# Hybrid decoder trunk, mixer projections: state space recurrence in steps of two tokens, and the input projection's units in another order with v, z and all six gates as three rounded products

## The chip, the cores and the metric

One core of one Trainium2 chip. The time is device microseconds of one execution. "Half step" below is one 128-token half of a 512-column projection; PE is TensorE, DVE VectorE, ACT ScalarE, POOL GpSimd, SP the queue that loads the weights.

## The reference

Two decoder layers on 256 tokens of width 1024, float32. Each layer first computes h = RMSNorm(x) and one wide projection of h, whose column blocks are:

```python
IN_SIZES = (MOBA_WIDTH, MOBA_WIDTH, MOBA_WIDTH,      # q, k, v of block attention, 512 each
            SSM_WIDTH,                               # u of the state space branch, 512
            GDN_WIDTH, GDN_WIDTH, GDN_WIDTH,         # q, k, v of gated DeltaNet before its convolution
            GDN_HEADS, GDN_HEADS, GDN_WIDTH,         # ab (8 columns), z
            D_MODEL, D_MODEL, D_MODEL)               # three merge gates, 6 blocks of 512
```

The state space branch keeps, for each of 32 groups of 16 channels, a complex diagonal state of 64:

```python
_, h = lax.associative_scan(combine, (a_elems, bu), axis=1)     # h_t = Lbar h_(t-1) + Bbar u_t
y = jnp.einsum('gnp,bsgp->bsgn', c_mat, h).real
y = y + d_skip * uf                                              # then GELU and GLU
```

Block attention and gated DeltaNet (GDN: a chunked delta rule with the inverse of a 64x64 unit lower triangle for each chunk and head) are the two other branches. The gated sum of the three goes through an output projection, then cross-attention and a feed-forward part follow (dense in layer 0, 8 experts in layer 1).

## The kernel before

The program is written out by hand: each engine has its own list of instructions, and semaphores join the lists. A list is worked through in order, so an instruction that waits holds back all that stand behind it on its engine.

**Weights.** SP loads 2 MB units of weights (24 a layer in the mixer, `mixer_units`, L74) into a ring of three slots; unit j is loaded when unit j - 3 has been multiplied (`multiplied`, L463). The first 14 units are column blocks of the input projection: u, q, k, v, z, gates 0 to 2, then the three convolution blocks QG, KG, VG, then the `NLATE` = 3 late units, gates 3 to 5.

**Two ways to multiply.** A float32 product of 128x128 by 128x512 is two PE instructions (`tokens_out` L2308, `features_out` L2295, `fill` L2365). A late unit (`late_gate` L2385) is multiplied as three rounded (fp32r) products: ACT writes the rounded weights (`unit_split_hi` L947), DVE the rest of them in place of the raw weights (`unit_split_lo` L1486), and h is parted in the same way (`h_rest` L1563, whose result lies over h itself, so that it waits until all float32 readers of h are done). A product is then h_hi x w_hi + h_lo x w_hi + h_hi x w_lo. Each unit is parted in four groups of 128x1024.

**State space loop.** 16 pairs of groups are worked in 8 steps g (`NGS` = 8). For each step PE makes B u into two PSUM banks of a pair that alternates (`s5_in` L2414), DVE turns it by a table of angles, scans it over 256 tokens and turns it back (L1618 to L1651), and PE multiplies the state by C (`s5_out` L2428). Tables are made four groups at a time by POOL (`angle_table` L812) and ACT (`table` L1006). After every second step DVE does `gelu_in(q-1)` (L1611), which waits for `s5_out` of two steps (y_read). PE's order around it is

```python
for g in range(NGS):
    s5_in(g)
    fill(4 + 2 * g)
    fill(5 + 2 * g)
    if g > 0:
        s5_out(g - 1)
s5_out(NGS - 1)
for f in range(F_LATE, NFILL):
    late_gate(f)
```

so that 16 half steps (v, z, gates 0 to 2, QG, KG, VG) stand in the loop and the three late units behind it. ACT takes each half step out of its bank, DVE turns q and k by position (L1592 to L1608) and scales the convolution's input (`conv_scale` L1556). Before the loop, `turn_b` (L2350) and `turn_c` transpose the matrices B and C, and `b_copy` and `c_copy` (L1016, L1022) bring them to SBUF.

**GDN inverse.** Six levels k double the size of the inverted blocks. Each level multiplies M_k by Z (L2612), ACT copies the product W (L1228), PE multiplies W with X and Z (L2621, L2624), DVE subtracts (L1866); one or two products for the cross-attention's values (`memory_values` L2548) stand between levels. M_k is masked by POOL (L855).

## Time and profile before

| | us |
|---|---|
| median of 3 runs (1904.75 to 1908.10) | 1907.74 |
| the profiled execution | 1899.46 |
| its span, first to last instruction | 1897.70 |
| PE busy / DVE busy / ACT busy / POOL busy | 1804.3 / 1410.7 / 1012.4 / 228.0 |
| state space loop and late units, layer 0 | 66.92 to 226.83 |
| the same, layer 1 | 700.58 to 860.48 |
| GDN inverse, layer 0 | 312.46 to 339.73 |
| expert part of layer 1 | from about 1110 to the end |

A line of the timeline reads: start, duration, engine, line of the kernel, operation, output<-inputs, shape, count of merged instructions, and in brackets the idle time before it and what ended it. Durations of one instruction reach beyond the start of the next where an engine is pipelined; the distance from start to start is what it costs.

### The profile page before, as it was taken

The numbers are of one execution on the slowest core, as the hardware profiler recorded it, in microseconds if no ns is written. First come the engines' busy times: TensorE is split into PE (matmuls) and PEld (weight loads), VectorE is DVE, ScalarE is ACT, GpSimd is POOL, SyncE is SP. The second block draws the span as 40 slices with busy tenths as digits, with TensorE's granted clock in tenths as the row PEclk, the third lists the DMA queues.
The fourth block names the chain that finished last, engine by engine and source line by source line (L and its number), as shares of the span: only waits on it lengthen the run. The fifth ranks groups of instructions, "written<-read, shape, count | busy, mean of one in ns | idle before, by whom it ended". The sixth has DMA issues, their size and how long they took to land.

```text
span 1897.7 us, 22679 instructions
## 1 busy us (share of the span) xinstructions
PE 1804.3 (95%) x9095; PEld 1369.5 (72%) x9095; DVE 1410.7 (74%) x1643; ACT 1012.4 (53%) x1164; POOL 228.0 (12%) x227
## 2 busy tenths in 40 slices
PE   7999999998999999998999879999999999999995
PEld 5447767576888744686766768787878787878784
DVE  4798778345555359986855469898989898989895
ACT  4231555345444312244714557777777777777773
POOL 9560001010000248100010010000000000000010
PEclk9999999999999999999999989999999999999998
DMA  7333422057553433343303469999999999999992
GB/s 246 133 133 133 178 89 90 1 208 246 199 183 105 150 133 133 133 155 112 131 4 144 145 249 391 379 390 359 390 361 390 361 390 355 391 354 392 353 392 86
DMA packets 204567, 434.85 MB, mean 229 GB/s; under 512 B 6888, under 2 KB 45936, under 8 KB 204464
## 3 DMA queue, kind: packets, MB, share of 16 engines
q1 hardware_dynamic: 196464, 414.20, 60.1%
q0 software_dynamic: 5136, 17.01, 2.5%
q10 hardware_dynamic: 2864, 2.23, 0.4%
q8 instruction: 69, 1.13, 0.2%
q14 instruction: 34, 0.28, 0.0%
HBM read 422.93 MB, written 10.49 MB: 228 GB/s over the span
## 4 chain that ended last, share of the span: by engine, by line
PE 80%; DVE 11%; ACT 5%; issue 2%; DMA 1%; ACTq 0%; POOL 0%; DVEq 0%; SPq 0%
PE bank L2749 14%; PE bank L2751 14%; PE bank L2750 14%; PE bank L2310 10%; PE bank L2381 4%; DVE split_e L1496 3%; PE bank L2303 2%; PE bank L2326 2%; PE bank L2330 2%; PE bank L2327 2%; PE bank L2551 2%; DVE phase L1745 1%; PE bank L2403 1%; PE bank L2409 1%; PE bank L2405 1%
## 5 line engine op out<-in xcount | busy, mean ns | idle before, releaser
L1496 DVE TENSOR_TENSOR split_e<-ring,split_e 128x2048 fp32r<-128x2048 f32 x264 | 600.4, 2289 | 50.9 <-ACT split_e L973 50.6
L973 ACT ACTIVATE split_e<-ring 128x2048 fp32r<-128x2048 f32 x264 | 503.8, 1919 | 160.6 <-PE bank L2751 159.1
L2749 PE MATMUL bank<-split_e,fx_e 128*128 128x512 f32 x704 | 278.8, 396 | 2.0 <-DVE fx_e L2163 2.0
L2751 PE MATMUL bank<-split_e,fx_e 128*128 128x512 f32 x704 | 274.7, 390 | 0.0
L2750 PE MATMUL bank<-split_e,fx_e 128*128 128x512 f32 x704 | 274.2, 389 | 0.0
L2310 PE MATMUL bank<-ring,hT 128*128 128x512 f32 x448 | 199.3, 603 | 3.1 <-DVE uT L1553 3.1
L2310 PEld LDWEIGHTS bank<-ring,hT 128*128 128x128 f32 x448 | 85.3, 193 | 108.8 <-issue 108.8
L2749 PEld LDWEIGHTS bank<-split_e,fx_e 128*128 128x128 f32 x704 | 132.2, 188 | 28.2 <-DVE fx_e L2163 2.2
L2751 PEld LDWEIGHTS bank<-split_e,fx_e 128*128 128x128 f32 x704 | 132.1, 188 | 28.2
L2750 PEld LDWEIGHTS bank<-split_e,fx_e 128*128 128x128 f32 x704 | 132.4, 188 | 26.3
L2749 PE MATMUL bank<-split_e,f_actT_e 128*128 128x512 f32 x352 | 138.7, 394 | 9.2 <-DVE f_actT_e L2171 9.2
L2750 PE MATMUL bank<-split_e,f_actT_e 128*128 128x512 f32 x352 | 137.1, 389 | 0.0
L2751 PE MATMUL bank<-split_e,f_actT_e 128*128 128x512 f32 x352 | 137.1, 389 | 0.0
L2749 PEld LDWEIGHTS bank<-split_e,f_actT_e 128*128 128x128 f32 x352 | 66.1, 188 | 26.1 <-DVE f_actT_e L2171 12.8
L2381 PE MATMUL bank<-hT,ring 128*128 128x256 f32 x384 | 84.5, 381 | 0.0
L2381 PEld LDWEIGHTS bank<-hT,ring 128*128 128x128 f32 x384 | 72.5, 190 | 11.6 <-issue 2.0
L2751 PEld LDWEIGHTS bank<-split_e,f_actT_e 128*128 128x128 f32 x352 | 66.1, 188 | 13.9
L2750 PEld LDWEIGHTS bank<-split_e,f_actT_e 128*128 128x128 f32 x352 | 66.1, 188 | 13.2
L1490 DVE TENSOR_TENSOR ring_r<-ring,ring_r 128x1024 fp32r<-128x1024 f32 x46 | 54.8, 1221 | 18.4 <-ACT ring_r L962 18.1
L2749 PE MATMUL bank<-split_mix,fx 128*128 128x512 f32 x168 | 66.5, 396 | 1.7 <-DVE phase L2106 1.7
L2751 PE MATMUL bank<-split_mix,fx 128*128 128x512 f32 x168 | 65.6, 390 | 0.0
L2750 PE MATMUL bank<-split_mix,fx 128*128 128x512 f32 x168 | 65.4, 389 | 0.0
(545 smaller groups left out, 3138.3 us busy)
## 6 DMA issues: line engine op xcount, KB each, us to landing
ring<-in_moe_w_gate SPq DMA_DIRECT2D x40, 2048.0 KB, 11.4
ring<-in_moe_w_up SPq DMA_DIRECT2D x40, 2048.0 KB, 11.3
ring<-in_moe_w_down SPq DMA_DIRECT2D x40, 2048.0 KB, 11.7
ring<-in_w_in SPq DMA_DIRECT2D x28, 2048.0 KB, 7.9
ring<-in_ffn_w_gate SPq DMA_DIRECT2D x11, 1024.0 KB, 5.4
ring<-in_ffn_w_up SPq DMA_DIRECT2D x11, 1024.0 KB, 8.0
ring<-in_ffn_w_down SPq DMA_DIRECT2D x11, 1024.0 KB, 8.7
ring<-in_ssm_w_glu SPq DMA_DIRECT2D x8, 1024.0 KB, 6.2
```

The costliest lines, as they stand in the source:

```text
L973: nc.scalar.activation(split_e[j % NBUF][:, HI, :], ring[:, s * PIECE + i * HGRP:s * PIECE + (i + 1) * HGRP], ACT.Copy).then_inc(split_hi, 1)
L1490: V.tensor_tensor(unit_lo(j, i), unit_raw(j, i), unit_hi(l, m).bitcast(F32), ALU.subtract).then_inc(split_lo, 1)
L1496: V.tensor_tensor(split_e[j % NBUF][:, LO, :], ring[:, s * PIECE + i * HGRP:s * PIECE + (i + 1) * HGRP], split_e[j % NBUF][:, HI, :].bitca ...
L2303: last = mm(B[banks[m // 2]][:, (m % 2) * SEQ:(m % 2 + 1) * SEQ], w[:, k, m * P:(m + 1) * P], src[:, k, :], start=k == 0, stop=k == KD - 1)
L2310: last = mm(B[bank][:, :], src[:, k, t * P:(t + 1) * P], w[:, k, n0:n0 + 512], start=k == 0, stop=k == kt - 1)
L2326: mm(B[bank][:, :], a[LO], hi, start=k == 0, stop=False)
L2327: freed = mm(B[bank][:, :], a[HI], hi, start=False, stop=False)
L2330: last = mm(B[bank][:, :], a[HI], lo, start=False, stop=k == 4 * per_group - 1)
L2381: last = mm(B[t][:, (m % 2) * SEQ:(m % 2 + 1) * SEQ], w[:, k, m * P:(m + 1) * P], hT[:, k, :], start=k == 0, stop=k == KD - 1)
L2749: mm(bank, a[HI], w[HI], start=first, stop=False)
L2750: mm(bank, a[HI], w[LO], start=False, stop=False)
L2751: return mm(bank, a[LO], w[HI], start=False, stop=last_one)
```

## The change

It does these things, in both layers unless said otherwise:

1. **Two tokens a step.** The scan runs over 128 pairs of tokens (`HS` = 128) with the decay squared. u is stored with the even tokens first and the odd ones behind. The input of a pair is B2 u_even + B u_odd, with B2 = Lbar B, a second matrix (`b_pad2`, `bT2`). States of odd tokens are read out with C; even tokens from the state before, with C2 = C Lbar (`cT2`, made by `output_matrix` on DVE), and with a direct term C B (`d_mat`, made by `direct` on PE and `d_copy` on ACT). Tables, scans and all DVE operations of a step are half as wide. B u now always goes to banks 6 and 7.
2. **Another order.** Units: u, q, k, QG, KG, VG, v, z, gates 0 to 5. `NLATE` is 8: v, z and the six gates are multiplied in three rounded passes, and five of the eight stand inside the loop, from step 3 on. The buffers of the rounded weights are four for all late units: group i of a unit is rounded when PE has used group i of the unit before.
3. **Layer 1 only:** q and k too are multiplied in three rounded passes (`early_hi`, `EARLY_HI`).
4. **GDN inverse:** level 0 takes M_0 and its product straight (X and Z begin as the identity), and level 5 leaves out the product that makes X.

```diff
@@ units
-    NLATE = 3
+    NLATE = 8
+    HS = 128
-        return ([in_cols(l, c) for c in (IN_U, 0, 512, 1024, IN_Z)]
-                + [in_cols(l, IN_GATE + 512 * g) for g in range(6 - NLATE)]
-                + [in_cols(l, c) for c in (IN_QG, IN_KG, IN_VG)]
-                + [in_cols(l, IN_GATE + 512 * g) for g in range(6 - NLATE, 6)]
+        return ([in_cols(l, c) for c in (IN_U, 0, 512, IN_QG, IN_KG, IN_VG, 1024, IN_Z)]
+                + [in_cols(l, IN_GATE + 512 * g) for g in range(6)]
@@ POOL
...
                 nc.gpsimd.memset(b_pad[:, :, :, :, :], 0.0).then_inc(pad_ready, 1)
+                nc.gpsimd.memset(b_pad2, 0.0).then_inc(pad_ready, 1)
@@ ACT
+            def early_hi():
+                for half in range(2):
+                    ks = slice(half * (KD // 2), (half + 1) * (KD // 2))
+                    nc.scalar.activation(e_r[HI][:, ks, :], hT[:, ks, :], ACT.Copy).then_inc(x_hi, 1)
+                    if U_LATE < j < U_GLU:
+                        act.wait_ge(split_used, unit_splits(l) + m - 4 + 1)
+                    early_hi()
+                    unit_split_hi(l, U_Q, range(4))
...
+                if l > 0:
+                    unit_split_hi(l, U_Q + 1, range(4))
-                b_copy(l)
+                b_copy(l, bT, 6, 1)
                 c_copy(l)
+                b_copy(l, bT2, 2, 3)
+                d_copy(l)
                 table(l, 0)
...
+                for n_ in range(NLATE):
+                    unit_split_hi(l, U_LATE + n_ + 1, range(4))
+                    late_out(n_)
+                    if n_ == 1:
+                        table(l, NQ - 1)
+                    if n_ == NGS - 4:
+                        for q in range(NQ):
+                            gelu_tanh(q)
@@ DVE, constants (each 128x32)
+            V.tensor_copy(AI, c_[6])
+            V.tensor_scalar(AR, c_[7], 1.0, None, ALU.add)
+            link(V.tensor_tensor(BCI, c_[11], c_[8], ALU.mult))
+            V.tensor_tensor(c_[8], BCR, AR, ALU.mult)
...
+            V.tensor_tensor(BCI2, c_[10], c_[11], ALU.add).then_inc(s5_const, 1)
@@ DVE, layer 1 before u: e_lo twice, then unit_split_lo(U_Q); after u: unit_split_lo(U_Q + 1)
+                input_matrix(0, b_pad, BCR, BCI)
+                input_matrix(1, b_pad2, BCR2, BCI2)
@@ DVE, end of a step of the loop
                     if g % 2 == 0:
                         dve.wait_ge(h_rot, n + 1)
                         if q > 0:
                             gelu_in(q - 1)
+                    if g == 0:
+                        output_matrix()
+                    if g == 2:
+                        unit_split_lo(l, U_LATE, range(4))
+                        dve.wait_ge(fill_ready, NFILL * l + F_LATE)
+                        h_rest(0)
+                        h_rest(1)
+                    if g >= 3:
+                        unit_split_lo(l, U_LATE + g - 2, range(4))
@@ DVE, GDN levels
+                        if k == 0:
...
+                            V.tensor_tensor(XZ[:, t, 0], XZ[:, t, 0], M_lvl[0][:, t], ALU.subtract)
...
+                            V.tensor_tensor(XZ[:, t, 1], XZ[:, t, 1], ps, ALU.subtract).then_inc(xz_ready, 1)
+                            continue
@@ PE
+                def late_unit(n_):
...
+                    for i in range(4):
+                        m = FIRST_SPLIT[j] + i
+                        pe.wait_ge(split_lo, unit_splits(l) + m + 1)
+                        if n_ == 0 and i % 2 == 0:
+                            pe.wait_ge(x_lo, xs_base(l) + X_H + i // 2 + 1)
+                        for t in range(NT):
+                            at, bank = slice(t * P, (t + 1) * P), B[2 * (n_ % 2) + t]
+                            for k in (2 * i, 2 * i + 1):
+                                hi, lo = (...)
+                                mm(bank[:, :], h_lo[:, k, at], hi, start=k == 0, stop=False)
+                                freed = mm(bank[:, :], h_hi(k)[:, at], hi, start=False, stop=False)
+                                last = mm(bank[:, :], h_hi(k)[:, at], lo, start=False, stop=k == KD - 1)
+                def direct():
+                    pe.wait_ge(bct_ready, 4 * l + 3)
+                    for q in range(NQ):
+                        for i in range(NQ):
+                            a = 32 * i
+                            for c in range(2):
+                                last = mm(B[2][a:a + 32, q * 32:(q + 1) * 32],
+                                          b_pad[:, c, NQ * q + i].rearrange("p g n -> p (g n)"), cT[:, c, q, a:a + 32],
+                                          start=c == 0, stop=c == 1)
                 def s5_in(g):
-                        pe.wait_ge(bu_read, NS5 * l + 2 * g - 2)
+                        pe.wait_ge(bu_read, NS5 * l + 2 * g)
                     for c in range(2):
                         for j in range(2):
-                            last = mm(s5_bank(g, j)[:, c * SEQ:(c + 1) * SEQ], bT[a:a + 32, c, q, :], uT[a:a + 32, q, :], ...)
+                            mm(s5_bank(g, j)[:, c * HS:(c + 1) * HS], bT2[a:a + 32, c, q, :], uT[a:a + 32, q, 0:HS],
+                               start=True, stop=False)
+                        for j in range(2):
+                            last = mm(s5_bank(g, j)[:, c * HS:(c + 1) * HS], bT[a:a + 32, c, q, :], uT[a:a + 32, q, HS:SEQ], ...)
                 def s5_out(g):
+                            mm(y[r_, 0:HS], cT2[:, c, q, r_], h[:, j, c, 0:HS], start=c == 0, stop=False)
+                        mm(y[r_, 0:HS], d_mat[r_, q, :], uT[r_, q, 0:HS], start=False, stop=True)
+                            last = mm(y[r_, HS:SEQ], cT[:, c, q, r_], h[:, j, c, 1:HS + 1], start=c == 0, stop=c == 1)
-                turn_b()
+                turn_b(0, b_pad, 6)
                 turn_c()
+                turn_b(1, b_pad2, 2)
                 fill(3)
+                direct()
                 for g in range(NGS):
                     s5_in(g)
-                    fill(4 + 2 * g)
-                    fill(5 + 2 * g)
+                    if g < 3:
+                        fill(4 + 2 * g)
+                        fill(5 + 2 * g)
+                    if g > 3:
+                        late_unit(g - 3)
                     if g > 0:
                         s5_out(g - 1)
+                    if g == 3:
+                        late_unit(0)
                 s5_out(NGS - 1)
-                for f in range(F_LATE, NFILL):
-                    late_gate(f)
+                for n_ in range(NGS - 3, NLATE):
+                    late_unit(n_)
@@ PE, GDN levels
-                    for t in range(NT):
+                    for t in range(NT) if k > 0 else ():
...
-                        for h, b, r_ in blocks:
+                        for h, b, r_ in blocks if k < 5 else ():
```

## Rows read from the trace of the kernel before

**Rows 1.** The page, part 4: the chain that ended last, by engine and line

```profile
PE 80%; DVE 11%; ACT 5%; issue 2%; DMA 1%; ACTq 0%; POOL 0%; DVEq 0%; SPq 0%
```

**Rows 2.** Busy time of each engine over loop and late units, layers 0 and 1

```profile
core 0: us, PE busy (x) PEld busy (x) DVE busy (x) ACT busy (x) POOL busy (x), PEclk, DMA share, GB/s
66.92:226.83 159.91, 159.91 (x625) 101.50 (x625) 141.57 (x198) 47.54 (x57) 55.53 (x24) 1.00 0.41 145
700.58:860.48 159.90, 159.90 (x625) 101.50 (x625) 142.04 (x198) 47.59 (x57) 55.96 (x24) 1.00 0.41 145
```

**Rows 3.** Timeline of PE in layer 0, loop and late units

```profile
58.22 1.04 PE L2354 MATMUL bank<-ident,b_pad 128*128 128x128 f32 x8
...
66.92 1.13 PE L2424 MATMUL bank<-uT,phase 32*128 32x256 f32 x8
67.99 14.00 PE L2310 MATMUL bank<-ring,hT 128*128 128x512 f32 x32
81.92 1.13 PE L2424 MATMUL bank<-uT,phase 32*128 32x256 f32 x8
...
96.91 1.06 PE L2438 MATMUL bank<-phase 128*32 128x256 f32 x8
```

**Rows 4.** The same timeline, first late product and what follows the last

```profile
194.05 0.50 PE L2403 MATMUL bank<-ring_r,m_hi 128*128 128x512 f32 x1
...
226.83 1.91 PE L2469 MATMUL bank<-ident,qk 128*128 128x128 f32 x16
```

**Rows 5.** Timeline of DVE in layer 0: gelu_in twice, and the parting

```profile
119.55 1.01 DVE L1616 TENSOR_SCALAR ring<-ring 128x256 f32<-128x256 f32 x1
...
178.15 0.48 DVE L1613 SCALAR_TENSOR_TENSOR yT<-uT,params,bank 128x256 f32<-128x256 f32 x1 [4.74 <-PE bank L2438]
178.67 0.42 DVE L1615 TENSOR_TENSOR ring<-yT 128x256 f32<-128x256 f32 x1
179.13 0.29 DVE L1616 TENSOR_SCALAR ring<-ring 128x256 f32<-128x256 f32 x1
...
179.80 0.68 DVE L1632 TENSOR_TENSOR phase<-bank,phase 128x512 f32<-128x512 f32 x1
...
190.10 4.63 DVE L1490 TENSOR_TENSOR ring_r<-ring,ring_r 128x1024 fp32r<-128x1024 f32 x4
194.65 1.22 DVE L1567 TENSOR_TENSOR merged_hi<-hT,m_hi 128x1024 fp32r<-128x1024 f32 x1
```

**Rows 6.** Timeline of POOL: first and last operation of one angle table

```profile
112.36 2.15 POOL L820 TENSOR_TENSOR ring<-s5c,steps 128x1024 f32<-128x1024 f32 x1 [4.55 <-ACT phase L1014]
...
130.70 1.29 POOL L827 TENSOR_SCALAR ring<-ring 128x1024 f32<-128x1024 f32 x1
```

**Rows 7.** Busy time by stretches, as rows 2: PE's two longest waits after the start

```profile
292.95:295.73 2.78, 0.00 (x2) 0.00 (x1) 2.71 (x4) 2.78 (x7) 0.00 (x0) 1.00 0.02 7
...
1095.40:1101.85 6.45, 0.00 (x0) 0.00 (x0) 4.00 (x28) 1.88 (x4) 0.00 (x0) 0.54 1.04 408
1101.85:1109.60 7.75, 6.49 (x30) 6.42 (x31) 3.34 (x7) 0.00 (x0) 0.00 (x0) 0.50 0.07 26
```

**Rows 8.** Timeline of PE in layer 1 before the loop

```profile
669.76 22.27 PE L2310 MATMUL bank<-ring,hT 128*128 128x512 f32 x48 [1.33 <-DVE uT L1553]
...
693.62 7.03 PE L2310 MATMUL bank<-ring,hT 128*128 128x512 f32 x16
```

**Rows 9.** Timeline of DVE in layer 0 ahead of the first half step

```profile
30.54 1.97 DVE L1541 TENSOR_SCALAR cosr<-cosr 128x64 f32<-128x64 f32 x1
```

**Rows 10.** Timeline of PE in layer 0: GDN inverse, levels 0 and 1

```profile
312.46 1.37 PE L2612 MATMUL bank<-uT,ring 64*64 64x64 f32 x32 [0.49 <-POOL ring L855]
313.71 0.68 PE L2621 MATMUL bank<-uT,ring 64*64 64x64 f32 x16
314.20 0.66 PE L2624 MATMUL bank<-ring,uT 64*64 64x64 f32 x16
...
315.73 1.12 PE L2551 MATMUL bank<-ring,hT 128*128 128x512 f32 x2
316.78 1.15 PE L2612 MATMUL bank<-uT,ring 64*64 64x64 f32 x32
```

**Rows 11.** The page, part 6: loads of the input projection's units

```profile
ring<-in_w_in SPq DMA_DIRECT2D x28, 2048.0 KB, 7.9
```

More of the change, by code:

```diff
@@ L228, in hybrid_trunk @@
         r5 = Region(phase, PH)
-        tab = [r5.take(NQ, 2, SEQ) for _ in range(2)]
+        r5.take(1024)
+        b_pad2 = r5.take(2, NS5, 2, 16)
         bT, cT = r5.take(2, NQ, P), r5.take(2, NQ, P)
-        s5_m1, s5_m2, s5_in_rot = (r5.take(2, 2, SEQ) for _ in range(3))
-        s5_h = [r5.take(2, 2, SEQ) for _ in range(2)]
-        ang, turns = spare_half(0, 0), spare_half(0, 1)
-        s_half = spare_half(1, 0)
+        bT2, cT2 = r5.take(2, NQ, P), r5.take(2, NQ, P)
+        d_mat = r5.take(NQ, 32)
+        s5_m1, s5_m2, s5_in_rot = (r5.take(2, 2, HS) for _ in range(3))
+        TAB1_AT = r5.at + NQ * 2 * HS
+        tab = [r5.take(NQ, 2, HS) for _ in range(2)]
+        s5_h = [r5.take(2, 2, HS + 1) for _ in range(2)]
+        ang, turns = spare_half(0, 0)[:, 0:NQ * HS], spare_half(0, 0)[:, NQ * HS:2 * NQ * HS]
+        s_half = spare_half(1, 0)[:, 0:NQ * HS]
         c_nat = spare_half(1, 1).rearrange("p (c q h s) -> p c q h s", c=2, q=NQ, h=2)
@@ L611, in s5_bank @@
         def s5_bank(g, j):
[L612 removed]
+            return B[6 + j]
         block = ctx.enter_context(nc.Block())
@@ L1546, in _ @@
                     rstd_diagonals(l)
+                for half in range(2) if l > 0 else ():
+                    dve.wait_ge(x_hi, xs_base(l) + X_E + half + 1)
+                    ks = slice(half * (KD // 2), (half + 1) * (KD // 2))
+                    V.tensor_tensor(e_r[LO][:, ks, :], hT[:, ks, :], e_r[HI][:, ks, :].bitcast(F32), ALU.subtract).then_inc(x_lo, 1)
+                if l > 0:
+                    unit_split_lo(l, U_Q, range(4))
                 dve.wait_ge(row_rstd_ps, l + 1)
@@ L1563, in h_rest @@
                 def h_rest(half):
-                    dve.wait_ge(x_hi, XS * l + X_H + half + 1)
+                    dve.wait_ge(x_hi, xs_base(l) + X_H + half + 1)
                     ks = slice(half * (KD // 2), (half + 1) * (KD // 2))
@@ L1589, in _, with input_matrix @@
-                last.then_inc(b_bar_ready, 1)
-                dve.wait_ge(b_bar_ready, l + 1)
+                at_l = slice(l * NS5, (l + 1) * NS5)
+                tb = [v.rearrange("p a b n -> p (a b n)")[:, j * 256:(j + 1) * 256].rearrange("p (t n) -> p t n", n=16)
+                      for v in (s5_m1, s5_m2) for j in range(2)]
+                def input_matrix(n_, pad, re, im):
+                    cr, ci = (v[:, at_l].unsqueeze(2).to_broadcast([P, NS5, 16]) for v in (re, im))
+                    V.tensor_tensor(tb[0], b_nat[:, 0], cr, ALU.mult)
+                    V.tensor_tensor(tb[1], b_nat[:, 1], ci, ALU.mult)
+                    V.tensor_tensor(tb[2], b_nat[:, 0], ci, ALU.mult)
+                    link(V.tensor_tensor(tb[3], b_nat[:, 1], cr, ALU.mult))
+                    dve.wait_ge(pad_ready, 3 * l + n_ + 1)
+                    for h in range(2):
+                        rows_ = slice(64 * h, 64 * (h + 1))
+                        V.tensor_tensor(pad[rows_, 0, :, h, :], tb[0][rows_], tb[1][rows_], ALU.subtract)
+                        last = V.tensor_tensor(pad[rows_, 1, :, h, :], tb[2][rows_], tb[3][rows_], ALU.add)
+                    last.then_inc(b_bar_ready, 1)
+                    dve.wait_ge(b_bar_ready, 2 * l + n_ + 1)
@@ L1672, in _ @@
                 V.scalar_tensor_tensor(y_lo, yflat, 0.5, y_hi.bitcast(F32), ALU.mult, ALU.subtract).then_inc(y_ready, 1)
-                for n_ in range(2, NLATE):
+                for n_ in range(NGS - 1, NLATE):
                     unit_split_lo(l, U_LATE + n_, range(4))
@@ L2366, in fill @@
                     j, t = U_Q + f // 2, f % 2
-                    if t == 0:
+                    if t == 0 and (f >= 4 or l == 0):
                         arrived(l, j)
```

286 lines of the change are left out of this document (143 added, 143 removed).

## The prediction

> **What bounds the kernel now.** I read the chain of waits first: 80% of it is PE [rows 1]. Then the busy times of the stretch that the change rebuilds: PE is busy for 159.91 of 159.91 us in layer 0, the same in layer 1, at the full clock, while DVE has 141.6 and ACT 47.5 of work [rows 2]. So in this stretch every microsecond of PE work counts, DVE is no bound but is not far from one, and a wait that is put on PE costs its whole length. The experts, behind the stretch, are not touched and should only move. The sum is made against the profiled execution (1899.46 us, span 1897.70), which is 8.3 under the median of the runs, 1907.74; I carry the difference over to the median.
>
> **1. Five more units in three rounded passes, each layer.** A float32 unit takes 81.92 - 67.99 = 13.93 us [rows 3]; the three rounded units took 226.83 - 194.05 = 32.78, so 10.93 each [rows 4]. v, z and gates 0 to 2 change: 5 x 3.00 = **-15.0 a layer**. QG, KG and VG stay float32; their move changes no duration. SP's loads keep their size, 7.9 us to landing [rows 11]: a slot is refilled one unit of 10.9 us and a group of 2.7 before ACT wants it, so I cost them at nothing. The new order within a unit (by groups, both halves together) is the same number of products.
>
> **2. Small products on PE, each layer.** s5_in is now 16 instructions of 128 columns, not 8 of 256: columns alike, 67.99 - 66.92 = 1.07 before [rows 3], 1.1 taken, 8 x 0.03 = 0.3. s5_out grows from 4 to 10 products, 1024 to 1280 columns: 0.99 (its 1.06 less the tail) becomes 1.24 by columns, 1.3 taken, 8 x 0.3 = 2.4. A second turn_b: 0.9, its row's 1.04 less the tail [rows 3]. `direct`: 64 instructions on 32x32 blocks; the nearest row, 32 on 64x64 blocks in 1.15 us [rows 10], gives 0.036 each, near 2.1. Together **+5.7 a layer**. The other end is a price per instruction (1.07 / 8 = 0.13): 2.1 for s5_in, 2.5 for s5_out, 8.6 for `direct`, some +20 a layer more. I take columns, since rows of 64 columns cost 0.036 and not 0.13. Less than nothing is excluded: the products are added.
>
> **3. DVE in the loop.** Its operations are half as wide: a 512-wide one takes 0.68, a 256-wide one 0.42 [rows 5]; a step falls from about 10 to under 6 us. To it come four partings of 1.14 a step, (194.65 - 190.10) / 4 [rows 5]: 4.6 + 6, plus gelu_in (179.80 - 178.15 = 1.65) every second step, stays below PE's 10.9 + 2.4. output_matrix (six 512-wide operations, 4 us) stands in step 0 beside 14 us of PE, and costs nothing; without that cover it would cost 4. ACT has 3.9 for a unit and 1.3 for its output, also beside PE.
>
> **4. But the order on DVE puts new waits on PE.** gelu_in(0) in step 2 waits for s5_out(1), which PE issues only after both half steps of step 2. Before, the same wait was 4.74 us at step 6 [rows 5] and nobody waited behind it; elsewhere DVE was late. Now the parting of the first rounded unit and h_rest are queued behind it, and late_unit(0) wants them at once. From the end of s5_out(1): gelu_in 1.65, four partings 4.55, first h_rest 1.22 = 7.4; PE has s5_in(3) and s5_out(2), 2.4, so it waits at least **5.0**. POOL adds to this. Its table of angles took 112.36 to 131.99 = 19.6 us [rows 6], so half as wide 9.8, and it starts when ACT has made table 2, 10.4 us into the step (1.1 + 7.0 for the half step, then 2.3); s5_out(1) ends at 1.1 + 13.9 + 1.3 = 16.3, so 3.9 us of POOL's work still lie beside the chain. Beside POOL the 0.29 operation L1616 took 1.01 [rows 5]. I add 2.2: a wait of 7.2. By the Trainium skill, SBUF — State Buffer, "Who interferes with whom", a DVE operation with both inputs in SBUF is held for the whole of a GpSimd operation that reads SBUF; the partings are such, and by that rule alone POOL's whole 3.9 would be added, 8.9. The row, a lengthening by 0.72, agrees in kind.
>
> gelu_in(1) and gelu_in(2) do the same at steps 4 and 6: the next unit's first group comes 1.65 + 1.22 after s5_out, PE has only s5_in, 1.1: 1.8 each, 3.6 in all. All later groups have 8.2 us (three groups of PE) for 2.4 us of ACT and DVE. Waits together: **+10.8 a layer** (8.6 to 12.5).
>
> **5. The clock.** After a wait of 2.78 us the granted clock stayed at 1.00, at 6.45 it fell to 0.54 and was 0.50 for the next 7.75 us, though there PE had thin work [rows 7]. A wait of 7.2 is longer than the one that lost the clock: 1.2 GHz of 2.4 for some us of late_unit(0). I take **+2.5 a layer**, between nothing and 3.9 (half of 7.75). The Trainium skill, TensorE: Matmul & The Clock Gate, "Why this matters for your kernels", warns of idle gaps between bursts in the same sense; by it the wait of part 4 always costs the clock, without it the sum would be 5.0 lower.
>
> Loop and late units together: -15.0 + 5.7 + 10.8 + 2.5 = **+4.0 a layer, +8.0**.
>
> **6. Layer 0, start.** Nine more 128x32 operations on DVE stand ahead of PE's first half step, and PE waits there. L1541 took 1.97 beside POOL [rows 9]; it may be shorter now, as POOL's operation is half as wide, while the new copy and tensor_scalar may be held likewise. **+1.0**, between 0 and 4 (two of them at 1.97). The second input matrix (eight 256-wide operations, 2.8) lies beside float32 half steps: nothing. POOL has one more memset and halved tables.
>
> **7. Layer 1, q and k in three passes.** Half steps of 5.47 instead of 6.97: 4 x 1.5 = -6.0. Three of them took 22.27, 1.4 more than 3 x 6.97, at the start [rows 8]; that stays. Before the first rotation of q, DVE now has four partings (4.55) and two input matrices (5.6) from 670.2 on, so it begins at 680.4 and ends at 682.9 (six operations of 0.42); the third half step wants its bank at 669.8 + 10.9 + 1.4 = 682.1: a wait of 0.8. The parts of h and q ahead of u lie beside PE's product of u and may slip by 0.3. **-4.9** (-6.0 to -2).
>
> **8. GDN inverse.** Level 0 loses ACT's copy and 64 of its 96 instructions: it took 316.78 - 312.46 = 4.32; now 1.37 and the 1.05 for the values remain, and DVE's two subtractions may add 0.2: -1.7. Level 5 loses 32 instructions, two times the 0.47 between 313.71 and 314.20: -0.9 [rows 10]. **-5.2** for both layers (-6 to -3).
>
> **Sum:** 8.0 + 1.0 - 4.9 - 5.2 = -1.1. The profiled execution would be at 1898.4 us, the median at **1906.6**. About 0.2%, 3.8 us, is what a measurement of this kernel can tell from no change.
>
> **Rivals.**
> A, short wait: POOL is out of the way and the clock holds, as it did after 2.78 us. Then the wait is 5.0 and part 5 is nothing: 2 x (2.2 + 2.5) = 9.4 less, 1897.2. For it: DVE's gelu_in has one operation of four with both inputs in SBUF. Against: 5.0 is nearer 6.45 than 2.78. 0.22.
> B, no waits at all: DVE hides parts 4 and 5: 26.6 less, 1880. Against it stands the list of instructions itself. 0.07.
> C, slower: s5_out mixes 128-row and 32-row blocks and `direct` changes block every four instructions; if blocks don't overlap, each costs more than its columns. Half way to the price per instruction, s5_out takes 1.95, s5_in 1.6 and `direct` 4.3: 7 x 0.65 + 5 x 0.5 + 2.2 = 9.2 a layer where no wait covers it, 1925. It decides for slower from about s5_out = 1.6. For it: fixed tails of 0.07 to 0.15 in rows 3. 0.18.
> D, the rounded units don't keep their pace: with one set of four buffers, a late ACT or DVE makes PE wait in every unit. At 1 us for each of the 7 later units: 14 more, 1921. Against: 5.8 us to spare in a group. 0.10.
> The forecast has 0.43, with its own range 1900 to 1912.
>
> **How the numbers follow.** Faster by over 0.2%: A, B and 0.10 of the forecast's 0.43, 0.39. Within: 0.28 of it and 0.03 of D, 0.31. Slower: 0.05 of it, C and 0.07 of D, 0.30. The range runs from below A, 1895, to 1921: left out are B and the upper half of C and a little of D, some 0.2.
>
> **What would show it.** In the profile after: a wait of PE of 5 to 9 us ahead of the first rounded product in each layer, put down to DVE's rest of h (L1567 before), DVE's own idle time ahead of gelu_in before it, a granted clock of 0.5 behind it; waits near 1.8 before the third and fifth rounded unit; rounded units at 10.9 us; s5_in near 1.1, s5_out near 1.3; the loop's stretch near 161 us a layer (159.9 - 15.0 + 2.7 + 10.8 + 2.5); the GDN inverse 2.6 us shorter. The forecast is wrong if PE doesn't wait there, if s5_out is over 1.6 us, or if the time lies outside the experts' common shift, that is if the expert part has another length than before.

## The result, and the profile after

The changed kernel takes 1912.69 us (median of 14 runs, 1909.04 to 1915.32); the kernel before, in the 14 runs taken with it, 1905.09. The ratio is 1.0039, 95% interval 1.0029 to 1.0048: slower by 7.6 us. Forecast were 1906.6 us and no clear change, with 0.39 for "faster", 0.31 for "within 0.2%" and 0.30 for "slower". The time lies inside the range of 1895 to 1921; the case that came was the least likely of the three. The first three runs of the kernel before, from which the forecast was made, were 2.7 us slower (1907.74) than the 14: against its own base the forecast was a change of -1.1 us, and +7.6 were measured. The profiled execution took 1912.5 us (span 1910.8, mean granted clock 0.977).

Loop and rounded units together, by stretches, columns as in [rows 2], of the changed kernel:

```profile
70.47:235.45 164.98, 153.72 (x871) 124.97 (x866) 121.59 (x225) 62.70 (x78) 29.53 (x24) 0.97 0.39 141
704.76:870.20 165.44, 154.18 (x871) 125.22 (x866) 121.60 (x225) 62.72 (x78) 29.48 (x24) 0.96 0.39 140
```

Before, PE was busy for all of 159.9 us here. Now it has less to do and yet the stretch is longer: in each layer some 11.3 us are waits, and the clock is no longer 1.00 throughout. DVE has lost 20 us of work and POOL 26; nothing of that reaches the end. Where the waits are is in PE's timeline, layer 0:

```profile
69.69 0.86 PE L2501 MATMUL bank<-phase,b_pad 128*32 128x32 f32 x64
70.47 0.49 PE L2515 MATMUL bank<-uT,phase 32*128 32x128 f32 x4
...
71.56 14.08 PE L2467 MATMUL bank<-hT,ring 128*128 128x256 f32 x64
85.57 0.49 PE L2515 MATMUL bank<-uT,phase 32*128 32x128 f32 x4
...
100.67 0.63 PE L2535 MATMUL bank<-phase 128*32 128x128 f32 x8
101.24 0.41 PE L2537 MATMUL bank<-uT,phase 32*32 32x128 f32 x4
101.57 0.63 PE L2540 MATMUL bank<-phase 128*32 128x128 f32 x8
102.14 0.49 PE L2515 MATMUL bank<-uT,phase 32*128 32x128 f32 x4
...
128.51 0.77 PE L2487 MATMUL bank<-ring_r,merged_hi 128*128 128x512 f32 x1 [7.18 <-DVE merged_hi L1614]
...
141.57 0.49 PE L2515 MATMUL bank<-uT,phase 32*128 32x128 f32 x4
...
142.66 0.50 PE L2487 MATMUL bank<-ring_r,merged_hi 128*128 128x512 f32 x1
...
153.76 0.63 PE L2535 MATMUL bank<-phase 128*32 128x128 f32 x8
...
158.42 0.47 PE L2487 MATMUL bank<-ring_r,merged_hi 128*128 128x512 f32 x1 [2.04 <-DVE ring_r L1519]
...
187.85 0.77 PE L2487 MATMUL bank<-ring_r,merged_hi 128*128 128x512 f32 x1 [2.04 <-DVE ring_r L1519]
```

The wait ahead of the first rounded unit is 7.18 us, and it waits for the rest of h, as forecast; the two before the third and fifth unit are 2.04. Of PE's own work: `direct` took 0.78 (69.69 to 70.47), s5_in 1.09, s5_out 1.47 (100.67 to 102.14), a rounded unit at full clock 11.10 (142.66 to 153.76), the first one 13.06 (128.51 to 141.57).

The last two s5_out stand back to back. Before, they took 1.01 us together (193.04 to 194.05 [rows 4]), no more than one alone (0.99); now they take 2.39 (200.28 to 202.67). Of the kernel before, the last half steps in the loop and this pair, then of the change the first line behind the pair:

```profile
179.03 14.08 PE L2381 MATMUL bank<-hT,ring 128*128 128x256 f32 x64
193.04 1.08 PE L2438 MATMUL bank<-phase 128*32 128x256 f32 x16
```

```profile
202.67 0.50 PE L2487 MATMUL bank<-ring_r,merged_hi 128*128 128x512 f32 x1
```

What DVE did ahead of the end of the wait of 7.18 us, and the ends of POOL's table of angles beside it (it answers to [rows 5, 6]):

```profile
118.89 0.48 DVE L1683 SCALAR_TENSOR_TENSOR yT<-uT,params,bank 128x256 f32<-128x256 f32 x1 [9.48 <-PE bank L2540]
119.40 0.63 DVE L1686 TENSOR_TENSOR ring<-yT 128x256 f32<-128x256 f32 x1
120.07 0.71 DVE L1687 TENSOR_SCALAR ring<-ring 128x256 f32<-128x256 f32 x1
120.82 1.45 DVE L1688 TENSOR_TENSOR ring<-ring,yT 128x256 f32<-128x256 f32 x1
122.19 2.76 DVE L1519 TENSOR_TENSOR ring_r<-ring,ring_r 128x1024 fp32r<-128x1024 f32 x2
124.88 2.35 DVE L1519 TENSOR_TENSOR ring_r<-ring,phase_r 128x1024 fp32r<-128x1024 f32 x2
127.15 1.21 DVE L1614 TENSOR_TENSOR merged_hi<-hT,m_hi 128x1024 fp32r<-128x1024 f32 x1
```

```profile
112.81 1.04 POOL L840 TENSOR_TENSOR ring<-s5c,steps 128x512 f32<-128x512 f32 x1 [15.44 <-ACT phase L1041]
...
122.08 0.67 POOL L847 TENSOR_SCALAR ring<-ring 128x512 f32<-128x512 f32 x1
```

DVE stands idle for 9.48 us at the head of its queue, waiting for s5_out(1), while the parting, whose inputs were there from ACT between 113.6 and 116.5 us, and the rest of h, which only has to wait for the last float32 half step (it ended at 117.24), lie behind. Then gelu_in takes 3.3 us beside POOL (118.89 to 122.19), not 1.65; the four partings take 5.0, not 4.55.

The clock, by stretches, same columns as above: a half step at the start, the long wait and the two parts of the unit behind it, the wait and start of the fifth unit.

```profile
34.82:40.60 5.78, 5.78 (x7) 2.47 (x8) 5.75 (x9) 0.00 (x0) 5.44 (x5) 0.50 0.52 156
121.32:128.51 7.19, 0.01 (x2) 0.03 (x1) 7.19 (x7) 0.00 (x0) 1.33 (x2) 0.82 0.42 160
128.51:132.74 4.23, 4.23 (x10) 3.37 (x11) 4.16 (x12) 0.00 (x0) 0.00 (x0) 0.50 0.00 0
132.74:141.57 8.83, 8.83 (x40) 7.02 (x39) 6.19 (x11) 3.31 (x4) 0.00 (x0) 1.00 0.00 0
185.81:187.85 2.04, 0.00 (x1) 0.03 (x1) 2.00 (x4) 0.00 (x0) 0.00 (x0) 0.88 1.04 400
187.85:191.00 3.15, 3.15 (x8) 2.53 (x9) 3.15 (x3) 0.00 (x0) 0.00 (x0) 0.54 0.74 282
```

So the clock of 2.4 GHz goes to 1.2 inside the long wait and comes back 4.2 us into the unit, which takes 13.06 us and not 11.10 (2.0 lost; 2.2 in layer 1). Around a wait of only 2.04 it was lost too at the fifth unit (12.43 against 11.12: 1.3; in layer 1 12.62: 1.5), and not at the third.

Outside the loop, PE in layer 1's start and in the inverse of layer 0 ([rows 8, 10]):

```profile
676.37 0.79 PE L2409 MATMUL bank<-q_hi,e_lo 128*128 128x512 f32 x1 [1.71 <-DVE uT L1598]
...
704.76 0.49 PE L2515 MATMUL bank<-uT,phase 32*128 32x128 f32 x4
```

```profile
321.05 1.37 PE L2719 MATMUL bank<-uT,ring 64*64 64x64 f32 x32 [0.49 <-POOL ring L876]
...
345.89 1.11 PE L2739 MATMUL bank<-uT,phase 64*128 64x64 f32 x16
```

28.39 us to the first s5_in, 2.43 less than before, with 1.65 for turn_b and `direct` in it: q and k give 4.1 here. The inverse takes 24.84, 2.4 less than the 27.20 before (the row that answers to 345.89 stood at 339.66).

### The profile page after: what moved, and what is told of

Read it like the earlier page. It is cut to its first block, busy times and chain, and to the rows that moved or that the text cites. A ratio compares the mean times of both kernels' runs of the same rounds, so it can differ in the third digit from the quotient of the medians.

```text
span 1910.8 us, 23760 instructions
## 1 busy us (share of the span) xinstructions
PE 1793.4 (94%) x9559; PEld 1426.3 (75%) x9559; DVE 1390.6 (73%) x1742; ACT 1044.5 (55%) x1208; POOL 166.2 (9%) x229
## 4 chain that ended last, share of the span: by engine, by line
PE 78%; DVE 12%; ACT 5%; issue 3%; DMA 1%; DVEq 0%; POOL 0%; ACTq 0%; SPq 0%
PE bank L2855 14%; PE bank L2857 14%; PE bank L2856 14%; PE bank L2467 4%; DVE split_e L1525 3%; PE bank L2487 3%; PE bank L2488 3%; PE bank L2491 3%; PE bank L2409 2%; PE bank L2386 2%; PE bank L2413 2%; PE bank L2410 2%; PE bank L2393 2%; PE bank L2658 1%; DVE ring_r L1519 1%
## 5 line engine op out<-in xcount | busy, mean ns | idle before, releaser
L2855 PEld LDWEIGHTS bank<-split_e,fx_e 128*128 128x128 f32 x704 | 132.3, 188 | 28.2 <-DVE fx_e L2246 2.2
L988 ACT ACTIVATE ring_r<-ring 128x1024 fp32r<-128x1024 f32 x71 | 73.5, 1056 | 99.4 <-PE bank L2488 85.3
L1519 DVE TENSOR_TENSOR ring_r<-ring,ring_r 128x1024 fp32r<-128x1024 f32 x71 | 86.9, 1251 | 22.0 <-ACT ring_r L988 21.8
L2856 PEld LDWEIGHTS bank<-split_e,f_actT_e 128*128 128x128 f32 x352 | 66.1, 188 | 13.1
L2487 PE MATMUL bank<-ring_r,merged_hi 128*128 128x512 f32 x128 | 54.5, 425 | 22.5 <-DVE merged_hi L1614 14.4
## 6 DMA issues: line engine op xcount, KB each, us to landing
ring<-in_moe_w_up SPq DMA_DIRECT2D x40, 2048.0 KB, 11.2
```

The costliest lines, as they stand in the source:

```text
L988: nc.scalar.activation(unit_hi(l, m), unit_raw(j, i), ACT.Copy).then_inc(split_hi, 1)
L1519: V.tensor_tensor(unit_lo(j, i), unit_raw(j, i), unit_hi(l, m).bitcast(F32), ALU.subtract).then_inc(split_lo, 1)
L2487: mm(bank[:, :], h_lo[:, k, at], hi, start=k == 0, stop=False)
L2855: mm(bank, a[HI], w[HI], start=first, stop=False)
L2856: mm(bank, a[HI], w[LO], start=False, stop=False)
```

## The experiments

Ratios are to runs of the kernel before on the same chip. Its medians there were 1903.95 to 1905.45 us, so a difference between the medians of two versions can hold up to 1.5 us of the chip.

### The order on DVE

**parting_first_once.** In step 2 of the loop on DVE:

```
-                        if q > 0:
+                        if q > 0 and g > 2:
                             gelu_in(q - 1)
 ...
                     if g == 2:
                         unit_split_lo(l, U_LATE, range(4))
                         dve.wait_ge(fill_ready, NFILL * l + F_LATE)
                         h_rest(0)
                         h_rest(1)
+                        gelu_in(0)
```

> Edit: in step 2 of the loop DVE does the parting of the first rounded unit and the rest of h before gelu_in(0), not behind it. Theory (order of DVE's queue): PE's wait of 7.18 us ahead of the first rounded product disappears in both layers, and with it the half clock behind it (the first rounded unit takes 13.06 us, 2.1 more than 10.9); the waits of 2.04 ahead of the third and fifth rounded unit stay. 2 x (7.2 + 2.1) = 18.6 less, a median near 1894. If only the wait goes and the clock is lost anyway: 14.4 less, 1898. Rival (DVE has too much work in this stretch): gelu_in only moves behind, step 3 of DVE comes later and PE waits as long at s5_out or at the second rounded unit: 1910 to 1914.

**parting_first_all.** The same in steps 4 and 6:

```
-                        if q > 0:
-                            gelu_in(q - 1)
 ...
                     if g >= 3:
                         unit_split_lo(l, U_LATE + g - 2, range(4))
+                    if g % 2 == 0 and q > 0:
+                        gelu_in(q - 1)
```

> Edit: as the one before, and in steps 4 and 6 too DVE does the parting of the next rounded unit before gelu_in. Theory (order): the two waits of 2.04 us go too, with the short stretch of half clock behind the one at the fifth rounded unit (some 1.5 us in each layer): another 2 x (4.1 + 1.5) = 11.2 less than with the first edit alone, near 1883. Rival: the parting's last group waits for ACT's copy, which waits for PE to have used the group of the unit before, so gelu_in comes later and delays s5_out(4) or step 5: the gain of this second edit is under 4 us.

Measured: 1899.54 us with the first edit (ratio to before 0.9960, interval 0.9944 to 0.9976), 1882.54 with both (0.9877, 0.9858 to 0.9897). PE ahead of the first and the third rounded unit with the first edit, then loop and rounded units of both layers with both edits, then what DVE did ahead of the first rounded unit there:

```profile
122.02 0.47 PE L2488 MATMUL bank<-ring_r,merged_hi 128*128 128x512 f32 x1 [0.74 <-DVE merged_hi L1614]
...
149.96 0.77 PE L2488 MATMUL bank<-ring_r,merged_hi 128*128 128x512 f32 x1 [2.04 <-DVE ring_r L1519]
```

```profile
68.73:219.79 151.06, 150.33 (x871) 122.34 (x866) 123.23 (x225) 62.72 (x78) 32.20 (x24) 1.00 0.44 154
689.71:840.77 151.06, 150.32 (x870) 122.34 (x865) 123.24 (x225) 62.70 (x78) 32.14 (x24) 1.00 0.44 154
```

```profile
112.04 2.77 DVE L1519 TENSOR_TENSOR ring_r<-ring,ring_r 128x1024 fp32r<-128x1024 f32 x2 [4.37 <-ACT ring_r L988]
114.73 3.20 DVE L1519 TENSOR_TENSOR ring_r<-ring,phase_r 128x1024 fp32r<-128x1024 f32 x2
117.86 2.31 DVE L1614 TENSOR_TENSOR merged_hi<-hT,m_hi 128x1024 fp32r<-128x1024 f32 x1
120.09 1.62 DVE L1614 TENSOR_TENSOR merged_hi<-hT,ring_r 128x1024 fp32r<-128x1024 f32 x1
```

The wait is nearly all a matter of order: the same DVE work, moved into DVE's own idle time, leaves 0.7 of the 7.18 us. That remainder fits POOL: the rest of h took 2.31 beside its table and 1.21 without. The first edit gave 13.1 us, nearer to "only the wait goes" (14.4) than to 18.6. The first rounded unit did keep its clock (11.09 and 11.07 us), but in this execution the third lost it (13.86 and 12.62 us), which kept it in the change (11.09 and 11.10): it now began at a granted clock of 0.51 (149.96 to 156.00). That removing the first wait brings this on is not shown: inverse_as_before below has the change's loop and its long wait, and there the third unit lost the clock in layer 0 (12.69) and kept it in layer 1 (11.08). With both edits no wait over 0.8 is left in the loop, the clock is 1.00 over both stretches, and a layer's loop takes 151.06, 8.85 less than before. The rival of each edit falls: the second gave 17 us, not under 4, and more than the 11.2 expected because the loss at the third unit went too. This is the version that beats both kernels: 1.2% faster than the kernel before.

### The clock apart from the wait

**wait_filled** and **wait_filled_short.** Products that nobody reads, in PE's queue ahead of the first rounded unit (14 of them, then 7):

```
                     if n_ == 0:
+                        for _ in range(14):
+                            mm(B[0][:, :], ident[:, :], uT[:, 0:2, :] ..., start=True, stop=True)
                         pe.wait_ge(x_hi, xs_base(l) + X_H + 2)
```

> Edit: the change, with 14 float32 products (ident by uT, 512 columns, some 0.43 us each, 6.1 us in all) that nobody reads, issued by PE ahead of the first rounded unit, where it waits 7.18 us for DVE. It tells the price of the half clock from that of the wait. Theory (the clock falls because PE stands idle): the wait shrinks to about 1.1 us, its end does not move, and the first rounded unit takes 10.9 us and not 13.06 (layer 0) or some 13.3 (layer 1): 2 x 2.2 = 4.4 less than the change, near 1908. Rival (the clock falls here for another reason, the thin products or the rounded ones themselves): the unit still takes 13, no change, 1912 to 1914.

> Edit: as wait_filled, with 7 of the products and not 14. There each product turned out to be two instructions of 0.44 us, 12.3 us for the 14, so that they outlasted the wait by 5 us in each layer; the clock stayed at 1.00 over the first rounded unit in both layers. 7 of them take 6.1 us and end inside the wait of 7.18. Theory (idleness costs the clock): the first rounded unit takes 10.9 us, 2.1 and 2.4 less than in the change, and nothing else moves: near 1908. Rival (something else by then, as the clock may be lost behind the next waits of 2.04 in its place): 1911 to 1914, with the half clock at the third or fifth rounded unit longer than in the change.

Measured: 1920.77 us (ratio 1.0092, 1.0074 to 1.0110) and 1910.28 (1.0038, 1.0021 to 1.0054). The first missed by my own sizing: the 14 products were 28 instructions and took 12.3 us. By stretches in the short one: the first rounded unit (without its last 0.19 us), then the start of the third.

```profile
128.30:139.20 10.90, 10.90 (x48) 8.90 (x48) 10.27 (x22) 3.18 (x3) 0.00 (x0) 1.00 0.00 0
156.25:159.10 2.85, 2.85 (x7) 2.27 (x8) 2.85 (x3) 0.00 (x0) 0.00 (x0) 0.51 0.85 323
```

The wait's end did not move (128.30 against 128.51) and the unit behind it ran at 1.00, 11.09 us in layer 0 and 11.07 in layer 1: so the half clock there came from PE's idleness and not from the kind of product. But 1910.3 is 2.4 under the change and not 4.4, and its interval (1.0021 to 1.0054) contains the change's 1.0039, so no gain is shown in the time. The two loops were only 0.7 and 0.6 us shorter than in the change: the third unit lost the clock in both layers (12.40 and 12.69 us), and the fifth as before.

Five traces hold the waits of 2.04 us: the change, wait_filled, wait_filled_short, parting_first_once and inverse_as_before, ten layers in all. The fifth unit lost the clock in all ten (12.4 to 12.7 us against 11.12). The third lost it in six of ten: in five of the six where the first unit ran at full clock, and in one of the four where it did not. That fits a loss that moves to the next wait, but with so few cases, and both outcomes on either side, it is not shown.

**order_and_filled** and **order_filled_short.** parting_first_all, with such products in the router's wait of 6.45 us and in the delta rule's waits of 2.8 (13 and 5 of them, then 6 and 2):

> Edit: parting_first_all (median 1882.5), with products that nobody reads in two other waits of PE: 5 of them (2.2 us) in each layer's wait of 2.8 us for the squares of the delta rule, 13 (5.6 us) in the wait of 6.45 us for the router's choice. If idleness costs the clock, the 7.7 us behind the router's wait (PE busy for 6.4 at 0.50) run at full clock, about 3 less, and the products behind the wait of 2.8, which lose 3.0 us in some executions and nothing in others, never lose it, on average 2 to 3 less for both layers: near 1877. Rival (thin work, 8 columns a product, counts as idle too): the clock falls ahead of the router's wait or behind it all the same, and at most the 2 to 3 of the delta rule are won; the fillers cost nothing while they end inside the waits.

> Edit: as order_and_filled, with 6 and not 13 products in the wait of 6.45 us and 2 and not 5 in each wait of 2.8 us; there they outlasted the waits by some 6.6 and 1.6 us, and the thin products behind the router's wait ran at full clock (32 of them in 3.81 us, against 5.77). Now they end inside the waits. Theory: 2.5 to 3 less behind the router's wait and on average 2 to 3 less in the delta rule: 1877 to 1878 against 1882.5. Rival (the clock is lost anyway, since thin products come ahead of and behind these waits): 1881 to 1884.

Measured: 1891.17 us (0.9931, 0.9915 to 0.9947) and 1882.42 (0.9886, 0.9872 to 0.9901), where parting_first_all had 1882.54. The long fillers outlast the waits; the short ones bring nothing. PE at the fillers and at the thin products behind them (8 columns each, then 128x128 ones), in the short one:

```profile
1076.99:1083.92 6.93, 6.93 (x15) 2.95 (x15) 4.33 (x28) 2.02 (x5) 0.00 (x0) 0.75 1.03 403
1085.00:1092.50 7.50, 5.53 (x33) 5.28 (x33) 1.84 (x6) 0.00 (x0) 0.00 (x0) 0.77 0.00 2
```

The clock falls at about 1078 us, 1 us into the fillers; at 0.75 on average they take 6.93 us and end after the router is ready, and the clock falls again in the thin work behind (at about 1088.6). My theory fell here: this stretch does not lose the clock by its one long wait alone, and of the two it is the rival (thin work ahead and behind) that the rows fit.

### Would the rounded units do without the pairs?

**dve_more.** parting_first_all, with more work on DVE in each step:

```
+                    for _ in range(10):
+                        link(V.tensor_tensor(scratch, uT[:, 0, :], uT[:, 1, :], ALU.mult))
```

> Edit: parting_first_all, with 10 more operations of 256 columns on DVE in each of the eight steps, each waited for, some 4.4 us: about what a recurrence over single tokens has more than one over pairs (10 us a step against 5.9). It tells whether the five rounded units could have been had without the pairs. Theory (DVE has little room once it parts a unit in every step): a step of DVE takes 4.6 + 6.3 + 4.4 and half of 1.6, 16.1 us, against 13.5 of PE, so PE waits some 2.5 us in each of five steps, with some lost clock: 20 to 30 more than 1882.5, near 1907, the gain over the kernel before gone. Rival (DVE's idle time takes it): under 5 more.

Measured: 1926.98 us (1.0124, 1.0105 to 1.0143), 44 more than without. PE's waits in layer 0's loop and by stretch:

```profile
PE bank L2490 <- DVE merged_hi L1615: 7.5, 1, 7.5
PE bank L2490 <- DVE ring_r L1520: 6.8, 5, 1.9
```

```profile
70.20:240.00 169.80, 155.44 (x857) 125.77 (x858) 156.59 (x305) 61.91 (x77) 30.03 (x24) 0.95 0.39 137
```

The theory holds and was too mild (20 to 30 us expected): 14.3 us of waits in a layer, and the clock with them (0.95). Half of it is one wait that I had not counted: the added operations in step 2 ran beside POOL's table (7.05 us for ten, 4.55 in the step before) and pushed the parting back by as much as gelu_in does in the change. DVE is busy for 156.6 of 169.8 us. The added operations stand for the one-token recurrence in number and width only; that recurrence itself was not built. As far as that stand-in goes, the pairs are what makes room on DVE for parting a unit in every step.

### The two other parts alone, and the kernel before once more

**inverse_as_before** and **order_inverse_before.** The inverse of the kernel before (level 0 and level 5 with all their products and ACT's copy), in the change and in parting_first_all; **order_qk_float32**, parting_first_all with q and k of layer 1 in float32:

```
-                    for t in range(NT) if k > 0 else ():
+                    for t in range(NT):
 ...
-                        for h, b, r_ in blocks if k < 5 else ():
+                        for h, b, r_ in blocks:
```

```
-                    if f < 4 and l > 0:
-                        last = split_out(l, j, t, e_r, ...)
-                    elif j < U_CONV:
+                    if j < U_CONV:
                         last = tokens_out(t, hT[:, :, :], t, w, KD, 0)
```

> Edit: the change with the inverse of the gated delta rule as before it (level 0 and level 5 with all products). By rows the change saved 2.4 us in layer 0 (the forecast said 2.6 a layer); so 2 x 2.4 = 4.8 more, near 1917.5. Second question, the clock: in the profile of the change three stretches of half clock stand in layer 1's delta rule, at 938, 1013 and 1023 us, which the profile of before does not have. If the shorter inverse brings them on, they are gone here, and the time is 4.8 more less 4.4, near 1913; if they hang on something else (where the stretches fall in time), they may stay.

> Edit: parting_first_all, with the inverse as in the kernel before. It prices part 4 alone where the loop loses no clock. By rows 2.4 a layer, 4.8 in all: near 1887.3. In inverse_as_before the same undoing cost nothing that could be measured (1912.7 against 1912.7); if that was chance of the clock, it shows here; rival (the shorter inverse loses by the clock, being thinner, what it saves in products): 1881 to 1884.

> Edit: parting_first_all, with q and k of layer 1 in float32 as in the kernel before. It prices part 3 alone. The forecast said 4.9 less for it; from the change's profile the half steps save 6.0 and give back 1.5 by a longer stretch of half clock at their start and 0.4 by a longer wait: 4.1. Expected 4 to 5 more than 1882.5, near 1887. Rival (the four half steps were not on the path, or the new wait and clock took all of it): under 1.5 more.

Measured: 1912.70 us (1.0031, 1.0020 to 1.0043), 1888.28 (0.9912, 0.9898 to 0.9926) and 1890.92 (0.9928, 0.9912 to 0.9943). On the version with the better order, the inverse is worth 5.7 us where rows give 4.8. On the change itself its undoing cost nothing (1912.70 against 1912.69, where 1917.5 was expected, or 1913 if the half clock went with it). The profile of that run shows layer 1's delta rule at full clock, where the change's profile has three stretches of half clock (from about 936, 1013 and 1023 us); whether the shorter inverse brought those on or chance did, one profile each can't tell, and it stays open. q and k are worth 8.4 us by the medians; by the two traces 5.5 (661.37 to 689.71 against 664.81 to 698.67). The rest was not traced; the mean granted clocks of the two profiles, 0.985 and 0.983, point to clock in other places.

**before_again.** No edit.

> No edit: the kernel before, for another profile of it. Its profiled execution was 1899.5 us where the median of 14 runs is 1905.1. Theory (the clock is what varies): a more typical execution shows one to three more stretches of half clock, by name in layer 1's delta rule behind PE's wait of 2.79 us, which cost 3.0 us in the change's profile; with them a span near 1903 to 1906 and a mean clock below 0.988. Rival (transfers or other engines vary): the same clock stretches as in the first profile and other waits.

Measured: 1905.07 us over 12 runs (ratio 0.9993, 0.9981 to 1.0004), its profile at span 1904.0 and mean clock 0.985. The delta rule's wait and what follows it, both layers, in this execution of the kernel before:

```profile
292.35:295.12 2.77, 0.00 (x0) 0.00 (x0) 2.70 (x4) 2.77 (x7) 0.00 (x0) 1.00 0.01 4
295.12:301.00 5.88, 5.88 (x10) 2.60 (x11) 5.77 (x14) 5.66 (x9) 0.00 (x0) 0.71 0.00 0
931.26:934.03 2.77, 0.00 (x1) 0.00 (x1) 2.70 (x4) 2.77 (x7) 0.00 (x0) 1.00 0.03 10
934.03:940.00 5.97, 5.97 (x10) 2.60 (x11) 5.86 (x15) 5.77 (x9) 0.00 (x0) 0.71 0.00 1
```

The waits are the same as in the first profile, to 0.1 us; the clock is not. The wait that kept the clock in [rows 7] loses it here, in both layers. The same in the changed kernel, where layer 0 kept it and layer 1 did not:

```profile
304.32:311.00 6.68, 6.68 (x19) 3.66 (x20) 6.57 (x16) 6.63 (x10) 0.00 (x0) 1.00 0.01 2
936.25:939.02 2.77, 0.00 (x0) 0.00 (x0) 2.70 (x4) 2.77 (x7) 0.00 (x0) 0.87 0.00 1
939.02:945.80 6.78, 6.78 (x9) 2.91 (x10) 6.67 (x16) 5.35 (x9) 0.00 (x0) 0.55 0.01 1
```

So the first profile of the kernel before, 5.6 us under its median, was an execution that had kept its clock. The two first profiles differ by 13.1 us of span, the medians by 7.6; the second profile of before against that of the change by 6.8.

## Why the prediction was wrong

By the steps of the prediction, what each measured in the change's profile, for both layers together (a plus is time that the forecast missed):

| step | forecast | measured | missed |
|---|---|---|---|
| 1 five rounded units | -30.0 | -28.2 | +1.8 |
| 2 s5_out | +4.8 | +8.6 | +3.8 |
| 2 `direct` | +4.2 | +1.6 | -2.6 |
| 2 s5_in, turn_b | +2.4 | +2.5 | +0.1 |
| 4 waits | +21.6 | +22.5 | +0.9 |
| 5 clock in the loop | +5.0 | +7.0 | +2.0 |
| 6 start of layer 0 | +1.0 | +1.9 | +0.9 |
| 7 q and k | -4.9 | -3.7 | +1.2 |
| 8 inverse | -5.2 | -4.8 | +0.4 |
| sum | -1.1 | +7.4 | +8.5 |

The clock in the loop is what the first and fifth rounded units took beyond 11.1 us: 3.3 and 3.7 in the two layers. With the other rows of the loop that gives its +5.1 and +5.5 us. The sum agrees with the medians (7.6); the 5.7 us by which the two first profiles differ more are half clock in layer 1's delta rule and behind it, from 936 us on, which the first profile of the kernel before does not have. The wait, the largest new cost, was forecast rightly. The steps that failed are sizes: s5_out (+3.8), the clock (+2.0) and the rounded units (+1.8), and eight of nine terms were too kind, if one of them by only 0.1. Only `direct` stood against them (-2.6), and that was luck: its price was wrong too. So a sum of -1.1 became +7.4 and went past the bound between "no change" and "slower".

**Step 4 held.** "A wait of 7.2" was 7.18 in both layers; "1.8 each" were 2.04. The profile puts it down to DVE's rest of h, DVE had its own idle time ahead of gelu_in, and the runs with another order removed all but 0.7 of it. The 2.2 added for POOL were sized well (gelu_in 1.65 more, the partings 0.4 more), though not from a like row: L1616 has one tensor as its input, and rival A counts one operation of gelu_in with both inputs in SBUF where there are two (L1686 and L1688). Rivals B and D did not come (there were waits; a rounded unit took 11.1 at full clock, and no wait stands within one).

**Step 2 failed in size, and s5_out is the term that missed most.** The forecast has it 0.3 dearer each, eight times a layer: +2.4. It measured +4.3 (6.94 us a layer before, 11.24 now). One s5_out, priced by its columns at 1.3, took 1.47: its three groups start 0.57, 0.33 and 0.57 apart, each some 0.08 more than by columns. And the eight are not alike: before, the last two took the time of one (1.01), now they take 2.39, 0.55 less than two. Rival C's threshold of 1.6 was not reached and the time was slower all the same. `direct` was the opposite: 0.78, 0.012 us an instruction, where 2.1 had been taken. That was no price by columns but one by instruction, from a row with twice the columns in each (64, not 32); and its blocks are 128x32, as its row shows, not 32x32. By columns it is as much as one s5_out of before, 2048 in 0.99 [rows 3], which would have been close. The Trainium skill, TensorEngine Tiling (Array Packing), "Key Properties", says that a change of tiling mode, other than a change of tile within a mode, drains the engine; the rows agree in kind, and no run here varied that alone.

**Step 1 left out the joints.** "10.93 each" came from three rounded units back to back [rows 4]. In the loop a rounded unit is preceded and followed by small products and takes 11.10 to 11.12 (142.66 to 153.76), so five of them save 14.1 us a layer and not 15.0. The three behind the loop still take 32.78 (202.67 to 235.45), and QG, KG and VG 14.01 each, before (179.03 to 193.04) as now (71.56 to 85.57). At full clock, in parting_first_all, this adds up: 159.9 - 14.1 + 4.3 + 0.2 + 0.7 = 151.0, and it took 151.06.

**Step 5 counted one loss of the clock and there were two.** "I take +2.5 a layer" stood for the long wait alone: it was 2.0 and 2.2 there. At the fifth unit, behind a wait of 2.04, another 1.3 and 1.5 were lost. I had taken 2.78 us as a wait that keeps the clock, from the one execution shown [rows 7]. That was the wrong reading of a row: it was chance, as before_again shows. The same holds for rival A, which rested on it. The sentence from the Trainium skill, TensorE: Matmul & The Clock Gate, "Why this matters for your kernels", that idle gaps between bursts cost the clock, held for the long wait, and the filled wait shows it.

**Steps 6 and 7**: PE's first half step in layer 0 began 0.98 later, as much as forecast, but not for the reason given: PE's wait for DVE there was 1.79 us against 1.72. PE reached that point 0.9 later, because the clock had fallen earlier, in the products ahead of it (`ab`: 4.35 us and not 3.63), and then it stayed down for some 10 us and not 7, which cost the half step the other 0.9. In parting_first_all, with the same code there, the half step began only 0.11 later than before; in parting_first_once and wait_filled_short the wait was 3.08 and 2.74. What DVE's added operations cost there varies, and one profile doesn't give it. q and k: the half steps were sized right, 5.5 by the traces when the clock behaves alike; in the change a longer half clock at their start took 1.5 of it, and the first wait grew by 0.4. The later wait of 0.8 that I had foreseen for a bank did not come there; in parting_first_all and wait_filled PE did wait for DVE ahead of k, 0.46 and 1.31 us.

**Step 8 held**: 2.4 a layer against 2.6.

## What to carry to other kernels

When an in-order engine gets new work in a loop, put what the bounding engine wants next ahead of anything that waits for the bounding engine itself; here two moved lines were worth 30 us, four times what the change had lost. Price a chain of several small terms with its joints and its clock, look whether neighbours of the old kernel overlapped before multiplying the price of one by their number, and don't trust the sign of a sum near zero: here eight of nine terms came out costlier than forecast. And take a second profile of the kernel before, when one execution lies 0.4% off its median: the rows that differ between the two are no evidence.

## What the runs showed of the hardware

- A wait of PE of 2.04 or 2.8 us, with small products around it, sometimes loses the clock and sometimes keeps it. The same kernel at the same place: 2.77 at 292 and 931 us, kept in one profile of the kernel before, lost in the other. The same loop: 2.04 ahead of the third rounded unit, kept in the change, lost in layer 0 of inverse_as_before. Ahead of the fifth unit 2.04 lost it in ten of ten (1.3 to 1.6 us each). The 0.7 left ahead of the first rounded unit in parting_first_all did not lose it.
- Filling one wait kept the clock behind it and still left the time nearly as it was (1910.3 against 1912.7), because it was lost at a later wait, 26 us on.
- A float32 product of 128x512 is two instructions of 0.44 us here (28 in 12.3), which I had taken for one.
- DVE beside POOL, both inputs in SBUF: an operation on 128x1024 took 2.31 us beside POOL's table and 1.21 after it; a 256-wide one (L1688) 1.45 instead of 0.42. One with a single tensor as input (L1687) took 0.71 instead of 0.29.
- Two s5_out of the kernel before, which write different partitions of the bank, took 1.01 us back to back where one takes 0.99; the same pair with the 32x32 group in each takes 2.39 where one takes 1.47.
- Products on 128x32 blocks with 32 columns run at 0.012 us an instruction (64 in 0.78), while s5_out, which changes between 128x32 and 32x32 blocks, takes 0.23 more than by columns, some 0.08 for each of its three groups.
